# ScalarE's first table load ahead of the first data, five first weight chunks loaded at once, and constants sent later, in a one-core kernel of three transformer layers

## The reference, cut to what matters

```python
def rmsnorm(x, g):
    xf = x.astype(jnp.float32)
    y = xf * lax.rsqrt(jnp.mean(xf * xf, axis=-1, keepdims=True) + EPS)
    return (y * g.astype(jnp.float32)).astype(x.dtype)

def retention_layer(h, g_norm, w_in, gn_gain, w_out):
    b, t, _ = h.shape
    proj = rmsnorm(h, g_norm) @ w_in            # 256x1024 @ 1024x6144
    q, k, v, gate = jnp.split(proj, [RET_QK_W, 2 * RET_QK_W, 2 * RET_QK_W + RET_V_W], axis=-1)
    ...
    q = rotary(heads(q, RET_QK_DIM), pos)
    k = rotary(heads(k, RET_QK_DIM), pos) * (RET_QK_DIM ** -0.5)
    o = retention_chunkwise(q, k, heads(v, RET_V_DIM))
    ...
    y = (jax.nn.silu(gate.astype(jnp.float32)) * o).astype(h.dtype) @ w_out
    return h + y
```

## Time and profile before

| | us |
|---|---|
| median of three runs | 896.41 |
| the profiled execution, its whole time | 896.33 |
| its span (first to last instruction) | 894.5 |
| TensorE busy | 870.6 |
| VectorE busy | 573.3 |
| ScalarE busy | 490.8 |
| GpSimd busy | 37.6 |
| mean granted TensorE clock | 0.99 |

### The profile page before, as it was taken

The page is one execution under the profiler, slowest core; times in us unless marked ns, Lnnn a source line. Parts: engine busy times, 40 slices in busy tenths (PEclk is TensorE's granted clock), DMA queues, the critical chain, the costliest instruction groups (busy, mean ns, idle before and its releaser), DMA issues.

```text
span 894.5 us, 12210 instructions
## 1 busy us (share of the span) xinstructions
PE 870.6 (97%) x4854; PEld 747.5 (84%) x4854; DVE 573.3 (64%) x897; ACT 490.8 (55%) x738; POOL 37.6 (4%) x49
## 2 busy tenths in 40 slices
PE   8999999999999999899999999999999999999995
PEld 7997887788799989899898878888888887888884
DVE  3895566545767763575585755697548538667675
ACT  5444444336555765568586745845544448756630
POOL 0000000000010000000000001100020000000002
PEclk9999999999999999899999999999999999999998
DMA  6965544534656775433423354675655526455411
GB/s 220 320 230 189 162 147 162 179 115 165 212 165 225 246 244 189 150 134 95 142 95 99 138 197 135 217 256 189 233 203 176 188 95 204 174 188 181 149 48 47
DMA packets 81495, 154.34 MB, mean 173 GB/s; under 512 B 3808, under 2 KB 12128, under 8 KB 81440
## 3 DMA queue, kind: packets, MB, share of 16 engines
q1 hardware_dynamic: 80080, 149.24, 49.3%
q0 software_dynamic: 1360, 4.33, 1.7%
HBM read 152.51 MB, written 1.05 MB: 172 GB/s over the span
## 4 chain that ended last, share of the span: by engine, by line
PE 90%; DVE 3%; ACT 3%; DMA 2%; issue 1%; POOL 0%; POOLq 0%; SPq 0%; DVEq 0%; ACTq 0%
PE acc L1986 11%; PE acc L1988 10%; PE acc L1987 10%; PE acc L1969 9%; PE acc L1971 9%; PE acc L1970 9%; PE acc L1995 7%; PE acc L1996 6%; PE acc L1997 6%; PE misc L2147 2%; PE misc L2015 2%; ACT whi L887 1%; DVE wlo L1326 1%; DMA raw<-in_ret_w_in_dram 1%; PE misc L2136 1%
## 5 line engine op out<-in xcount | busy, mean ns | idle before, releaser
L1326 DVE TENSOR_TENSOR wlo<-raw,whi 128x2048 fp32r<-128x2048 f32 (+3 forms) x147 | 316.9, 2174 | 94.5 <-ACT whi L887 93.8
L887 ACT ACTIVATE whi<-raw 128x2048 fp32r<-128x2048 f32 (+3 forms) x147 | 267.3, 1826 | 156.6 <-PE acc L1988 79.3
L1986 PE MATMUL acc<-whi,xhiA 128*128 128x512 f32 x272 | 109.2, 402 | 0.0
L1988 PE MATMUL acc<-whi,xloA 128*128 128x512 f32 x272 | 106.1, 390 | 0.0
L1987 PE MATMUL acc<-wlo,xhiA 128*128 128x512 f32 x272 | 106.0, 390 | 0.0
L1969 PE MATMUL acc<-whi,xhiA 128*128 128x512 f32 x240 | 93.8, 391 | 0.0
L1971 PE MATMUL acc<-whi,xloA 128*128 128x512 f32 x240 | 93.5, 389 | 0.0
L1970 PE MATMUL acc<-wlo,xhiA 128*128 128x512 f32 x240 | 93.4, 389 | 0.0
L1995 PE MATMUL acc<-xhiC,whi 128*128 128x256 f32 x256 | 74.3, 290 | 3.5 <-issue 3.5
L1996 PE MATMUL acc<-xloC,whi 128*128 128x256 f32 x256 | 73.6, 287 | 0.0
L1997 PE MATMUL acc<-xhiC,wlo 128*128 128x256 f32 x256 | 73.5, 287 | 0.0
(11 more groups left out here) (294 smaller groups left out, 1710.2 us busy)
## 6 DMA issues: line engine op xcount, KB each, us to landing
raw<-in_w_in_dram SPq DMA_DIRECT2D x36, 1024.0 KB, 5.2
raw<-in_ret_w_in_dram SPq DMA_DIRECT2D x21, 1024.0 KB, 5.2
raw<-in_nsa_w_in_dram SPq DMA_DIRECT2D x16, 1024.0 KB, 5.3
raw<-in_kv_w_dram SPq DMA_DIRECT2D x12, 1024.0 KB, 5.3
raw<-in_ret_w_out_dram SPq DMA_DIRECT2D x8, 1024.0 KB, 5.0
raw<-in_ple_w_gate_dram SPq DMA_DIRECT2D x8, 1024.0 KB, 5.6
raw<-in_nsa_w_out_dram SPq DMA_DIRECT2D x8, 1024.0 KB, 5.1
raw<-in_cmp_w_k_dram SPq DMA_DIRECT2D x4, 1024.0 KB, 5.5
```

The costliest lines, as they stand in the source:

```text
L887: nc.scalar.activation(whi[plan.slot[c]][:, 0:size], raw[c % RAW_SLOTS][:, 0:size], ACT.Copy).then_inc(hi_done, 1)
L1326: nc.vector.tensor_tensor(wlo[plan.slot[c]][:, 0:size], raw[c % RAW_SLOTS][:, 0:size], whi[plan.slot[c]][:, 0:size].bitcast(F32), ALU.subt ...
L1986: nc.tensor.matmul(o, xh, hi[:, j, off:off + cols], start=start, stop=False)
L1988: ins = nc.tensor.matmul(o, xl, hi[:, j, off:off + cols], start=False, stop=stop)
```

## The change

- ScalarE's queue now begins with the transfer of `head`; SyncE sends x's halves one behind the other. ScalarE then runs one copy of a single column (`gains` to `ssq`, which is written again later), and its table load stands ahead of that copy instead of the first `xhi`.
- The five chunks of `ret_q0` (2048 KB together) share two raw buffers: chunks 0 to 2 lie side by side in buffer 0, chunks 3 and 4 in buffer 1, each with a semaphore of its own (`first_in`). None of them waits for a buffer. Chunk 5 goes to buffer 2, again without a wait. Chunk 6 waits for `wlo` of chunk 2, chunk 7 for that of chunk 4, and every later chunk for that of the chunk three before.
- `ret_k0` is no longer cut finer: it is chunks 5 and 6, whole ones, and all later chunk numbers fall by one (146 chunks instead of 147).
- In `norm_hi` and `norm_lo` chunk 0 stands ahead of pair 0.
- The constants are sent behind chunk 10 instead of chunk 8.

```diff
+    def raws(self):
+        self.raw, self.raw_before = [], []
+        small = len(FIRST_CUTS) - 1
+        last_in = [None] * RAW_SLOTS
+        at = 0
+        for c, (_, _, ks, width, *_) in enumerate(self.chunks):
+            if c < small:
+                i, at = at // CH, at + len(ks) * width
+                self.raw.append((i, at - len(ks) * width - i * CH, 1))
+                self.raw_before.append(None)
+            else:
+                i = (c - 3) % RAW_SLOTS
+                self.raw.append((i, 0, 1 + (c - (5, 6, 7)[(i + 1) % 3]) // RAW_SLOTS))
+                self.raw_before.append(last_in[i])
+            last_in[i] = c
...
-        std(f"ret_k{i}", rw, D + i * HALF, KD, "tr", "A", cuts=(0, 2, 4, 8) if i == 0 else None)
+        std(f"ret_k{i}", rw, D + i * HALF, KD, "tr", "A")
...
                 sp.dma_start(h[:, m], w["x"][0, m * P:m * P + P]).then_inc(x_in[m], 16)
-                if m == 0:
-                    sp.dma_start(head[:], w["head"]).then_inc(head_in, 16)
             for c, (key, src, ks, width, *_) in enumerate(plan.chunks):
-                if c >= RAW_SLOTS:
-                    sp.wait_ge(lo_done, c - RAW_SLOTS + 1)
+                if plan.raw_before[c] is not None:
+                    sp.wait_ge(lo_done, plan.raw_before[c] + 1)
                 n = len(ks) * width
-                dst = raw[c % RAW_SLOTS][:, 0:n].rearrange("p (k n) -> p k n", n=width)
-                sp.dma_start(dst, src).then_inc(raw_in[c % RAW_SLOTS], 16)
+                sp.dma_start(raw_part(c).rearrange("p (k n) -> p k n", n=width), src).then_inc(raw_sem(c), 16)
                 if c == 5:
                     sp.dma_start(rbuf[:, 0:trig_w], ret_consts[:, 0:trig_w]).then_inc(trig_in, 16)
                 if c == 8:
                     sp.dma_start(rbuf[:, trig_w:], ret_consts[:, trig_w:]).then_inc(decay_in, 16)
+                if c == 10:
                     sp.dma_start(cbuf[:], consts).then_inc(const_in, 16)
...
             def norm_hi(n, s, pairs=range(4)):
+                if n == "ret":
+                    split_until(1)
                 for j in pairs:
                     before_misc("norm", n, j, ahead=0 if n == "ret" else 1 + j // 2)
                     norm_hi_pair(n, n, s, j)
                     if n == "ret":
-                        split_until(j + 2 if j else 2)
+                        split_until(j + 2)
...
+            act.dma_start(head[:], w["head"]).then_inc(head_in, 16)
+            act.wait_ge(warm_set, 1)
+            nc.scalar.activation(ssq[:, 0, 0:1], gains[:, 0, 0:1], ACT.Copy)
             act.wait_ge(head_in, 16)
             norm_hi("ret", "A")
```

More of the change, by code:

```diff
@@ L429, in xt_needed @@
         return ("norm", "ret", (FIRST_CUTS[i] + j) // 2)
-    if name == "ret_k0":
-        return ("norm", "ret", (0, 1, 2)[i] + j // 2)
     half = min(i, 1)
@@ L464, in build @@
     plan.slots(plan.chunk_no[("kc", 0)], plan.upto[("T", NG - 1, 1, HPG - 1)] + AHEAD)
+    plan.raws()
     xt_no = xt_order()
@@ L610, in build @@
         raw_in = [sem(f"raw_in{i}") for i in range(RAW_SLOTS)]
+        first_in = [sem(f"first_in{i}") for i in range(len(FIRST_CUTS) - 1)]
         hi_done = sem("hi_done")
@@ L753, in build, with raw_part, raw_sem @@
                      "ln_g": (w["ln_g_2"], 1), "ln_b": (w["ln_b_2"], 0)}
+        def raw_part(c):
+            i, at, _ = plan.raw[c]
+            return raw[i][:, at:at + len(plan.chunks[c][2]) * plan.chunks[c][3]]
+        def raw_sem(c):
+            return first_in[c] if c < len(first_in) else raw_in[plan.raw[c][0]]
         def cmp_x(half):
@@ L882, in split_until @@
                     size = len(ks) * width
-                    act.wait_ge(raw_in[c % RAW_SLOTS], 16 * (c // RAW_SLOTS + 1))
+                    act.wait_ge(raw_sem(c), 16 * plan.raw[c][2])
                     if plan.slot_before[c] is not None:
                         act.wait_ge(chunk_used, plan.used_up[plan.slot_before[c]])
-                    nc.scalar.activation(whi[plan.slot[c]][:, 0:size], raw[c % RAW_SLOTS][:, 0:size],
-                                         ACT.Copy).then_inc(hi_done, 1)
+                    nc.scalar.activation(whi[plan.slot[c]][:, 0:size], raw_part(c), ACT.Copy).then_inc(hi_done, 1)
                     done[0] += 1
@@ L1325, in split_until @@
                     dve.wait_ge(hi_done, c + 1)
-                    nc.vector.tensor_tensor(wlo[plan.slot[c]][:, 0:size], raw[c % RAW_SLOTS][:, 0:size],
+                    nc.vector.tensor_tensor(wlo[plan.slot[c]][:, 0:size], raw_part(c),
                                             whi[plan.slot[c]][:, 0:size].bitcast(F32),
```

## The result

| | before | changed |
|---|---|---|
| median, us | 895.83 (4 runs, 894.86 to 897.64) | 888.92 (4 runs, 888.12 to 889.90) |
| ratio of the runs | | 0.992, 95% interval 0.9906 to 0.9934 |
| profiled execution, us (span) | 896.33 (894.5) | 888.96 (887.1) |
| mean granted TensorE clock | 0.99 | 0.995 |

6.9 us faster. The forecast was 893.5, with 892.4 to 895.4 as its range: right in direction, wrong by more than half of the gain.

The account below looks back on a forecast made before the run. TensorE, busy 97% of the span, was taken as the bound, so only its early waits could be won: 1.47 + 0.75 + 0.63 = 2.85 us off 896.33 gave 893.5, range 892.4 to 895.4.

Parts of the forecast that it names:

- The beginning: Before 37 us: earlier table load and chunks start ret_k0 sooner and remove two later stalls; 2.85 us in all.
- the rivals of late transfers: First 20 us: chunk 5 lands late; 894.7 us (late transfers, 18%) or 897.7 (slower; 5% together with nothing gained).
- the two later stalls: TensorE's waits at 30.43 and 36.91 us in the kernel before; both go, worth 0.75 and 0.63 us.
- Constants and the saved chunk boundary: Constants sent later and one chunk fewer: worth nothing, as constants are first read some 70 us later.
- A gain at 36.91: After 36.91 us no view shows TensorE waiting until 150 us, so a gain there should reach the end whole.
- The slow rival: Ahead of ret_k0: at 250 GB/s uncut chunk 5 lands at 19.7, 4.2 us late; 897.7 us, 3% for slower.
- the other estimate: Chunk 5's landing from chunk 9's slow rate: 0.74 + 1.4 + 13.0 = 15.2 us, with 0.3 us to spare.

Follow-up runs that it names:

- experiment 1: Kernel before with one line changed: the four whi slots handed out in order 3, 0, 1, 2, the changed kernel's phase; 893.2 us, ratio 0.9975.
- experiment 2: Changed kernel with the whi slots handed out in order 1, 2, 3, 0, restoring the old order of splits; 891.87 us, ratio 0.9965.
- experiment 9: Changed kernel with the constants (320 KB) sent behind chunk 8 again; 890.12 us, ratio 0.9935.
- experiment 3: Changed kernel with ret_k0 cut into 2, 2 and 4 row tiles again, slots kept in the changed kernel's phase; 888.89 us, ratio 0.9932.
- experiment 4: Changed kernel with VectorE doing wlo of chunk 5 between the norm's two sums instead of behind the root; 888.36 us, ratio 0.9931.
- experiment 5: Changed kernel with both head edits undone: head between x's halves on SyncE's queue, no early copy; 892.3 us, ratio 0.9964.
- experiment 6: Changed kernel without the early copy of one column, head still on ScalarE's queue; 891.19 us, ratio 0.9951.
- experiment 7: Changed kernel without the early copy, with 7 instead of 3 matmuls on ones ahead of the first real matmul; 890.45 us, ratio 0.9943.
- experiment 8: Changed kernel with chunk 0 behind the operand's first pair on ScalarE and VectorE, as before; 889.07 us, ratio 0.9929.
- experiment 10: Kernel before with only the two head edits (early copy and table load, head on ScalarE's queue); 893.68 us, ratio 0.9979.
- experiment 11: Changed kernel with VectorE doing wlo of chunk 68 ahead of the first group's scores instead of behind them; 884.15 us, ratio 0.9872.

## Why the prediction was wrong

**Right.** The beginning as a mechanism: the table off the path, no idle ScalarE ahead of chunks 3 and 4, `ret_k0` still held by the uncut chunk's `wlo`, no wait ahead of chunks 6 and 7. The transfers kept up: chunks 3, 4 and 5 landed at about 10.7, 12.0 and 14.75, where 10.9, 12.2 and 14.9 were forecast, and the rivals of late transfers fell. The trace shows no drain behind a table load: in the changed kernel the first one ends at 2.46 and the copy starts at 2.47, and of its 29 loads 17 have the next instruction 0.01 us behind them.

**Too small.** The beginning brought 3.45 us instead of 2.85. Chunk 0 was begun at 6.77 instead of 7.12, which with some tenths of shorter gaps moves `ret_k0` by 0.45; the two later stalls gave 1.53 instead of 1.38. Chunk 0's landing isn't a fixed number: ScalarE began chunk 0, or the table load ahead of it, at 6.58 to 7.73 in nine executions with `head` on ScalarE's queue, and at 8.07 in the one with it on SyncE's. The two rows could not show such a spread.

**The step that failed** is the term that was put at nothing, "Constants and the saved chunk boundary are worth nothing", and with it "A gain at 36.91 should therefore reach the end whole". I followed the change through the numbers of chunks in the first 40 us and took the rest as a shift. The renumbering moved a split at the 240th microsecond and brought 2.9 us in the profiled executions (2.70 by experiment 1's trace, 0.1 where experiment 2 undoes it). For the constants themselves nothing is what the runs show, within 0.2 us by the trace (experiment 9). It could be found without a run, since the rows of order differ there. It could be priced too: TensorE's wait of 2.67 us stands in the view of waits from 60 to 300 us of the kernel before, which no step of the prediction uses, and the chunk's 1.9 and 2.3 us stand in the timelines ahead of it. That the rows which matter lie in the first 60 us was the same error.

**Not in the sum at all** was the clock. I said that it is at 1.00 and left it there, because the 1.91 us idle ahead of the first matmul had cost nothing in the one execution I had. In three others 1.84 to 2.08 us there were followed by a clock of 0.50, which made the first block 1.5 us longer and `ret_k0` about 0.8 us later. The early table load is thus worth 2.3 us by the medians (2.1 by the traces), not 1.28: it shortens the wait to 0.73 us. The remaining 1.03 us between the profiled executions, at 370 us, I take for chance of this clock: the changed kernel and experiments 3 to 8 had the short low stretch there, the kernel before and experiments 1, 2, 9 and 10 the long one, and no edit touches that place. With one trace for each kernel it isn't shown.

The sum in the traces is 3.45 + 2.91 + 1.05 = 7.41 us, 1.03 of the last term at 370 us. The medians give 6.9.

**Slips beside the sum.** The slices around 4 to 7.5 us moved 246 to 393 GB/s, not 280 to 390, and those with 348 to 414 stand at 13 to 17 us, not at 12 to 16. The slow rival's landing at 250 GB/s comes to 19.2 with the start that the other estimate uses (0.74 + 1.4 + 17.1), not 19.7; its time would be 897.2 and its limit about 262 GB/s. Neither changes the forecast.

## What to carry to other kernels

When a change adds or removes an item that a planner numbers, compare the order of instructions to the very end, without line numbers, before counting anything as a shift; a look-ahead rule over slots can move work anywhere. Price an idle stretch of TensorE with what its clock does around it: here 2.7 us idle cost 4.1, and 3.5 cost 5.1 or 6.1. And where the trace puts a wait down to "issue", look for an instruction of another engine that ends just then: at 366 us it was a `wlo` that stood behind work of its own engine, as moving it showed; at 36.91 another `wlo` ended at that moment, which no run tested.

## What the runs showed of the hardware

- Executions lose a different amount around the same 3.52 us wait. The granted clock fell to its lower level in all traces that have the wait, and the lead over before differs by 1.0 to 1.2 us between those with the short and the long low stretch. The kernels with the wait spread over 1.0 us (4 runs) to 5.3 us (11 runs), the two without it over 1.1 and 0.6 us (4 runs each), which is too few runs for a verdict. The Trainium skill ("TensorE: Matmul & The Clock Gate", "Part 1: The HAM clock gate") says that the number of slow matmuls at a kernel's start varies from run to run of the same kernel. These traces show a spread of 1.0 us in mid-kernel, between kernels that have one trace each. For one kernel against itself there is only the mean granted clock: 0.992 to 0.997 in the changed kernel's four runs.
- In these executions about 2 us idle ahead of the first real matmul went with a full clock in one profiled execution (1.91 us) and with 1.2 GHz for about 3 us in three (1.84, 2.07, 2.08). Idleness of 0.22 to 1.72 us there was never followed by it (changed kernel and experiments 3, 4, 7, 8, 10 and 11).
- In experiment 1 x's second half landed at 7.86, and the wait of 2.04 us ahead of it was followed by a clock of 0.50 from 9 to 11 us. It cost nothing that shows: TensorE ran only transposes and products of ones then, and the first real matmul came 1.23 us later than in the kernel before, as x did (7.86 against 6.6).
